# Two of eight convolution chunks leave VectorE in a decoder block: ScalarE makes the taps' products, GpSimd adds them

## What is computed

```python
y = lax.conv_general_dilated(u, conv_w[:, None, :], window_strides=(1,),
    padding=[(CONV_KERNEL - 1, 0)], dimension_numbers=('NWC', 'WIO', 'NWC'),
    feature_group_count=CONV_WIDTH)      # CONV_KERNEL = 31 taps
y = y + conv_b
y = layer_norm(y, ln_g, ln_b)            # over the 1024 channels
return jax.nn.silu(y)
```

## Time and profile before

| | |
|---|---|
| time, median of 3 runs | 1834.55 us (1831.73 to 1835.55) |
| span of the profiled execution | 1831.1 us |
| PE busy | 1786.4 us, 98% |
| VectorE busy | 1586.1 us, 87% |
| ScalarE busy | 826.3 us, 45% |
| GpSimd busy | 208.4 us, 11% |
| memory traffic | 618 MB, mean 337 GB/s |

### The profile page before, as it was taken

The page is one execution under the profiler, slowest core; times in us unless marked ns, Lnnn a source line. Parts: engine busy times, 40 slices in busy tenths (PEclk is TensorE's granted clock), DMA queues, the critical chain, the costliest instruction groups (busy, mean ns, idle before and its releaser), DMA issues.

```text
span 1831.1 us, 28933 instructions
## 1 busy us (share of the span) xinstructions
PE 1786.4 (98%) x9874; PEld 1564.5 (85%) x9874; DVE 1586.1 (87%) x2605; ACT 826.3 (45%) x1187; POOL 208.4 (11%) x193
## 2 busy tenths in 40 slices
PE   6999999998999999999999999999999999999998
PEld 6878888444999999999999999998888888888886
DVE  4668899966678999999999999998888888888887
ACT  3011222302645554333566666664555555554544
POOL 1000000110000000110122111121111111111110
PEclk9999999999999999999999999999999999999999
DMA  9998766799686677999999999999999999999994
GB/s 386 421 421 344 274 251 252 288 422 372 230 322 249 237 241 249 374 329 332 330 353 365 362 358 361 365 361 374 385 369 368 365 375 361 375 365 367 373 371 202
DMA packets 98193, 617.98 MB, mean 337 GB/s; under 512 B 13233, under 2 KB 21969, under 8 KB 26449
## 3 DMA queue, kind: packets, MB, share of 16 engines
q1 hardware_dynamic: 61456, 415.26, 59.2%
q0 software_dynamic: 25408, 184.58, 26.5%
q10 hardware_dynamic: 11266, 17.32, 2.6%
HBM read 600.26 MB, written 16.79 MB: 337 GB/s over the span
## 4 chain that ended last, share of the span: by engine, by line
PE 77%; DVE 10%; DMA 8%; issue 3%; ACT 1%; DVEq 0%; SPq 0%; ACTq 0%
PE ps L1310 31%; PE ps L960 14%; PE ps L967 9%; DMA raw<-in_w_ada 6%; PE ps L1005 6%; PE ps L1114 5%; PE ps L1168 4%; PE ps L1262 2%; PE ps L1016 2%; DVE big L1390 2%; DVE raw L1415 1%; DVE w_low L1368 1%; DMA big<-in_w_gate_f 1%; DVE big L1471 1%; DMA raw<-in_peer_v 1%
## 5 line engine op out<-in xcount | busy, mean ns | idle before, releaser
L673 ACT ACTIVATE w_hi<-raw 128x1024 fp32r<-128x1024 f32 x520 | 552.0, 1062 | 494.8 <-PE ps L1310 241.4
L1368 DVE TENSOR_TENSOR w_low<-raw,w_hi 128x1024 fp32r<-128x1024 f32 x520 | 633.4, 1223 | 92.4 <-ACT w_hi L673 85.6
L1310 PE MATMUL ps<-w_hi,a 128*128 128x512 f32 x1536 | 390.9, 390 | 2.0 <-ACT w_hi L673 2.0
L960 PE MATMUL ps<-a,w_hi 128*128 128x384 f32 x1856 | 374.1, 342 | 0.9 <-issue 0.8
L1310 PEld LDWEIGHTS ps<-w_hi,a 128*128 128x128 f32 x1536 | 288.7, 188 | 62.7 <-ACT stage L774 1.6
L960 PEld LDWEIGHTS ps<-a,w_hi 128*128 128x128 f32 x1856 | 316.0, 189 | 1.9 <-issue 1.7
L1310 PE MATMUL ps<-w_low,a 128*128 128x512 f32 x1024 | 274.8, 390 | 0.0
L967 PEld LDWEIGHTS ps<-a,w_low 128*128 128x128 f32 x1856 | 237.9, 191 | 9.2 <-DVE w_low L1368 9.0
L967 PE MATMUL ps<-a,w_low 128*128 128x192 f32 x1856 | 241.5, 272 | 3.8 <-DVE w_low L1368 3.5
L1310 PEld LDWEIGHTS ps<-w_low,a 128*128 128x128 f32 x1024 | 192.5, 188 | 40.8 <-DVE w_low L1368 0.7
L1415 DVE CUSTOM_DVE_ANT_0 raw<-raw,big 128x2048 f32<-128x2048 f32 x64 | 146.2, 2290 | 65.9 <-DMA raw<-in_w_ada 63.3
(11 more groups left out here) (225 smaller groups left out, 1670.2 us busy)
## 6 DMA issues: line engine op xcount, KB each, us to landing
raw<-in_peer_u SPq DMA_DIRECT2D x128, 1024.0 KB
raw<-in_peer_v SPq DMA_DIRECT2D x128, 1024.0 KB
early<-in_w_front SPq DMA_DIRECT2D x56, 1024.0 KB, 9.0
raw<-in_w_ada POOLq DMA_DIRECT2D x48, 1024.0 KB, 8.2
raw<-in_w_ada SPq DMA_DIRECT2D x32, 1024.0 KB, 12.6
raw<-in_peer_wq SPq DMA_DIRECT2D x16, 1024.0 KB
big<-in_w_gate_f SPq DMA_DIRECT2D x16, 1024.0 KB, 7.4
gel_saved<-stage ACTq DMA_DIRECT2D x64, 192.0 KB
```

Of the source, the lines that this page charges most:

```text
L673: act.activation(w_hi[:, h % 2, :], raw[:, s % RING, :], ACT.Copy).then_inc(hi_ready, 1)
L960: done = pe.matmul(ps[:, b % 2, 0:2 * TD].rearrange("p (m t) -> p m t", m=2), w_hi[:, ph.nth(j) % 2, k * P:(k + 1) * P], a_pair[:, kc, :, ...
L1310: done = pe.matmul(ps[:, 4 * tt + 2 * (j % 2) + n, :], a, w[:, n * 512:(n + 1) * 512], start=i is None and blk == 0 and m in (0, 2), stop= ...
L1368: dve.tensor_tensor(w_low[:, s % RING, :], raw[:, s % RING, :], w_hi[:, h % 2, :].bitcast(F32), ALU.subtract).then_inc(lo_ready, 1)
```

## The change

Chunks 6 and 7 are made by ScalarE and GpSimd. ScalarE makes for each tap two products of 128 x 256 (`upad` shifted, times the weight per channel), tap 0 straight into `convT` with the bias, the others into a ring of four `products` tiles of 128 x 512; `two_taps(m)` stands at four places of each pair. GpSimd adds a product tile to the two chunks (`add_tap`, a `tensor_tensor` of 128 x 512, 30 of them), each add behind the issue of a certain modulation block (`TAPS_BEHIND`). VectorE does the first six chunks in the pairs 0 to 2, and in the last pair ten column sums in place of 62 taps and one column sum. `MOD_ORDER` brings their blocks early. `sum_channels` waits for GpSimd's last add, too. The column sums behind the pairs are nine fewer.

```diff
-for p in range(PAIRS):
+for p in range(PAIRS - 1):
...
+SUMS_LAST_PAIR = (2, 2, 2, 2, 2)
+FFN_AT_LAST = [PAIRS - 1 + sum(SUMS_LAST_PAIR[:n]) for n in range(len(SUMS_LAST_PAIR) + 1)]
+FFN_EARLY = FFN_AT_LAST[-1]
+MOD_ORDER += [A_GATE + 12] + [A_FFN + k for k in range(FFN_AT_LAST[0], FFN_AT_LAST[2])] + [A_GATE + 13]
+MOD_ORDER += [A_FFN + k for k in range(FFN_AT_LAST[2], FFN_AT_LAST[4])] + [A_GATE + 14]
+MOD_ORDER += [A_FFN + k for k in range(FFN_AT_LAST[4], FFN_EARLY)] + [A_GATE + 15]
...
+DVE_CHUNKS = CONV_CHUNKS - 2
+TAPS_BEHIND = ((2, 4, 5, 5, 6) + (8, 9, 11, 11, 14) + (16, 17, 18, 20, 22) +
+               (24, 24, 24, 26, 26, 26, 26, 26, 28, 28, 28, 28, 28, 30))
...
+        products = region(25984, 4, 2 * T)
...
+            last_chans = convT[:, DVE_CHUNKS:CONV_CHUNKS, :].rearrange("p a b -> p (a b)")
+
+            def add_tap(j):
+
+                gp.wait_ge(tap_product, 2 * (j + 1))
+                if j > 1:
+                    gp.wait_ge(tap_added, j - 1)
+                gp.tensor_tensor(last_chans, last_chans, products[:, j % 4, :], ALU.add).then_inc(tap_added, 1)
+
             for n in range(A_GATE, N_A):
                 gp.wait_ge(mod_used, max(A_GATE, n - SLOTS + 1))
                 gp.dma_start(mod_slots[n % SLOTS], w_ada[n]).then_inc(mod_in[n % SLOTS], 16)
+                nth = n - A_GATE - SLOTS
+                if 0 <= nth < len(TAPS_BEHIND):
+                    for j in range(TAPS_BEHIND[nth - 1] if nth else 0, TAPS_BEHIND[nth]):
+                        add_tap(j + 1)
...
+            def tap_products(j):
+
+                if j == 0:
+                    act.wait_ge(glu_ready, CONV_CHUNKS)
+                    act.wait_ge(late_in, 16 * N_LATE)
+                if j >= 5:
+                    act.wait_ge(tap_added, j - 4)
+                for n in range(2):
+                    ch = DVE_CHUNKS + n
+                    if j == 0:
+                        act.activation(convT[:, ch, :], upad[:, ch, 0:T], ACT.Identity, bias=conv_v[:, 0, ch:ch + 1],
+                                       scale=conv_wt[:, ch, 0:1]).then_inc(tap_product, 1)
+                    else:
+                        act.activation(products[:, j % 4, n * T:(n + 1) * T], upad[:, ch, j:j + T], ACT.Copy,
+                                       scale=conv_wt[:, ch, j:j + 1]).then_inc(tap_product, 1)
+
+            def two_taps(m):
+
+                for j in range(2 * m, min(2 * m + 2, TAPS)):
+                    tap_products(j)
...
             for p in range(PAIRS):
                 put_qk(p, 0)
+                two_taps(4 * p)
                 if p:
                     put_aT(2 * p - 2)
                     exps(2 * p - 1)
...
+                two_taps(4 * p + 1)
                 put_qk(p, 2)
...
+                two_taps(4 * p + 2)
                 put_qk(p, 3)
...
                 exps(2 * p)
+                two_taps(4 * p + 3)
                 put_v(p)
...
-            for p in range(1, PAIRS):
+            for p in range(1, PAIRS - 1):
...
+            head_combine(HEADS - 4)
+            head_scores(HEADS - 3)
+            gate_step(12)
+            sums_last_pair(0)
+            head_combine(HEADS - 3)
+            sums_last_pair(1)
+            gate_step(13)
+            heads_variance(PAIRS - 2)
+            sums_last_pair(2)
+            heads_scale(PAIRS - 2)
+            sums_last_pair(3)
+            gate_step(14)
+            sums_last_pair(4)
+            head_scores(HEADS - 2)
+            gate_step(15)
...
-            dve.wait_ge(tap, TAPS * CONV_CHUNKS)
+            dve.wait_ge(tap, TAPS * DVE_CHUNKS)
+            dve.wait_ge(tap_added, TAPS - 1)
             sum_channels(convT)
-            column_sums(4, 5)
+            column_sums(13, 14)
```

More of the change, by code:

```diff
@@ L82 @@
 MOD_ORDER = list(range(A_GATE))
-for p in range(PAIRS):
+for p in range(PAIRS - 1):
     MOD_ORDER += [A_GATE + 4 * p, A_GATE + 4 * p + 1] + [A_FFN + p] * (p > 0)
     MOD_ORDER += [A_GATE + 4 * p + 2] + [A_FFN + p] * (p == 0) + [A_GATE + 4 * p + 3]
+SUMS_LAST_PAIR = (2, 2, 2, 2, 2)
[4 more added lines that the diff above has]
+MOD_ORDER += [A_FFN + k for k in range(FFN_AT_LAST[4], FFN_EARLY)] + [A_GATE + 15]
 MOD_GATES = len(MOD_ORDER)
-MOD_ORDER += range(A_FFN + PAIRS, N_A)
+MOD_ORDER += range(A_FFN + FFN_EARLY, N_A)
 MOD_AT = {nth: n for n, nth in enumerate(MOD_ORDER)}
+DVE_CHUNKS = CONV_CHUNKS - 2
+TAPS_BEHIND = ((2, 4, 5, 5, 6) + (8, 9, 11, 11, 14) + (16, 17, 18, 20, 22) +
+               (24, 24, 24, 26, 26, 26, 26, 26, 28, 28, 28, 28, 28, 30))
 GATE_AT = [7, 7] + [min(2 * g + 8, g + 22) for g in range(2, KC)]
@@ L280, in build_block @@
         glu_done, sig_ready, glu_ready, tap = sem("glu_done"), sem("sig_ready"), sem("glu_ready"), sem("tap")
+        tap_product, tap_added = sem("tap_product"), sem("tap_added")
         qk_evac, v_evac = sem("qk_evac"), sem("v_evac")
@@ L1552, in _, with sums_last_pair @@
                 gate_step(g0 + 3)
+            def sums_last_pair(n):
+                column_sums(FFN_AT_LAST[n], FFN_AT_LAST[n + 1])
+            head_combine(HEADS - 4)
[13 more added lines that the diff above has]
+            gate_step(15)
             head_combine(HEADS - 2)
             head_scores(HEADS - 1)
-            dve.wait_ge(tap, TAPS * CONV_CHUNKS)
+            dve.wait_ge(tap, TAPS * DVE_CHUNKS)
+            dve.wait_ge(tap_added, TAPS - 1)
             sum_channels(convT)
-            column_sums(4, 5)
+            column_sums(13, 14)
             dve.wait_ge(ln_sum, 1)
@@ L1566, in _ @@
             sum_channels(conv_sq)
-            column_sums(5, 7)
+            column_sums(14, 16)
             dve.wait_ge(ln_sum, 2)
@@ L1570, in _ @@
                 .then_inc(ln_var, 1)
-            column_sums(7, 8)
+            column_sums(16, 17)
             dve.wait_ge(ln_root, 1)
@@ L1577, in _ @@
                 dve.tensor_tensor(chans, chans, bcast_t(stat[:, 1, :], 4), ALU.mult).then_inc(ln_n, 1)
-            column_sums(8, 11)
+            column_sums(17, 20)
             heads_variance(PAIRS - 1)
-            column_sums(11, 12)
+            column_sums(20, 21)
             heads_scale(PAIRS - 1)
-            column_sums(12, 19)
+            column_sums(21, 26)
             dve.wait_ge(gate_sum_ready, 1)
@@ L1588, in _ @@
                     .then_inc(gate_made, 1)
-            column_sums(19, 22)
+            column_sums(26, 29)
             dve.wait_ge(gate_made, 4)
@@ L1602, in _ @@
                 gate_mix(0, n)
-            column_sums(22, 2 * KC - 1)
+            column_sums(29, 2 * KC - 1)
             def gate_tile(tt):
```

## The result

The changed kernel takes 1856.88 us (median; 1855.69 to 1858.76), the kernel before 1833.69 us (1831.73 to 1835.55) on the same chips: a ratio of 1.0125, 95% interval 1.0113 to 1.0137. It is 23 us slower. The profiled execution spans 1855.9 us, 24.8 more than before's.

The account below looks back on a forecast made before the run. PE was taken to pace, with the time hanging on when VectorE reaches the channel sum. 28.4 us of contention less 14.0 us free made 14.4 us: span 1845.5, median 1849.0 us, range 1833 to 1858.

Parts of the forecast that it names:

- What sets the end: When VectorE reaches the channel sum, then 327.7 us; a microsecond later there is, to first order, one at the end.
- work behind 352 us is covered: 352 to 444 us: PE runs without a stop, so nine column sums fewer on VectorE are worth nothing by themselves.
- Contention: Pairs, 28 adds ahead of VectorE's last gate step: 26.2 us of blocking plus 2.2 us of broken overlap, 28.4 us.
- DMA: Last pair, 14 w_ada blocks instead of 5: VectorE waits 0 to 3.2 us, counting only where it is not late anyway.
- turns on the read path: While a GpSimd add runs, no two-operand VectorE instruction runs; 1849.0 us, chance 0.62.
- What VectorE may lose: Ahead of the channel sum: 9.3 us of waits plus 4.7 us saved, so 14.0 us of added VectorE time are free.
- not slower if VectorE is late: VectorE's waits for PE or ScalarE, 9.3 us in all, absorb a delay since those engines are not slower.
- the 4.7 us of relief: Last pair: 24.6 us of taps leave VectorE and 19.9 us of column sums come in, saving 4.7 us.
- ScalarE and GpSimd's queue: Pairs: product groups ahead of `exps` and `put_v(3)`, and adds behind w_ada issues, are hidden and cost nothing.
- Side by side: Rival: no slowdown of VectorE or GpSimd by each other, no change, say 1834.5 us; chance 0.21.
- GpSimd is the one that waits: Rival: adds get in only in VectorE's waits and one-operand steps, delaying w_ada and add 30; 1838.5 us, chance 0.11.
- What would show it: Signs: longer taps in 150 to 320 us, PE waiting at L1031 or L1042, channel sum near 342 us, VectorE's waits gone.

Follow-up runs that it names:

- the kernel with neither: Changed kernel without GpSimd's additions and with one column sum in the last pair, ScalarE's products kept: 1833.11 us, 0.9999 against the kernel before.
- the kernel that only writes: Changed kernel with GpSimd's 30 additions replaced by fills of the same 128x512 tile, waits kept: 1842.81 us, 1.005 against the kernel before.
- the single instructions: Small kernel of its own, single VectorE instructions issued while GpSimd adds run: two SBUF operands 1.47 instead of 0.48 us.
- The kernel with late sums: Changed kernel with adds kept, one column sum in the last pair and nine back behind the pairs: 1846.51 us, 1.0069 against the kernel before.
- the kernel without adds: Changed kernel without GpSimd's 30 additions, ScalarE's products and ten early column sums kept: 1843.11 us, 1.0053 against the kernel before.
- the small kernel: Separate kernel of VectorE tap streams with GpSimd adds released into them: an add asked after the 12th of 24 taps stood 5.79 us.

## Why the prediction was right, and where it was not

**What sets the end: right.** Everything behind the channel sum moved as one. It starts 23.8 us later, PE's waits of 1.87 and 0.69 us come back at the same distance, and the span is 24.8 us longer; the last microsecond I did not look for. It holds less well for small shifts: 1.3 us earlier in the kernel with neither gave no shorter span. That work behind 352 us is covered holds as well.

**The sum was too small**: 14.4 us late at the channel sum against 23.8. Three terms are mis-sized, and two of them nearly cancel: contention 6.7 us too large, the free time 6.1 us too large. What is left is DMA.

*Contention, 28.4 us forecast, 21.7 measured.* That is each VectorE group's growth of the mean times its count in 139 to 351 us: taps 6.3, gate steps 0.8, column sums 1.1, `head_combine`'s small instructions 10.2 (L1548 from 287 to 950 ns, x7, is 4.6 of it; L1551 2.65, L1546 2.4, L1540 0.55), L1558 2.3, L1584 1.1. It makes 0.78 us an add for 28 adds, against 1.01 in the forecast. The mechanism is right: turns on the read path, shown by the kernel that only writes (484 ns a tap again) and by the single instructions. The add was taken as 1.04 us and is 1.26; the part of it that VectorE pays was taken as 0.9 and is 0.62 (0.78 of 1.26). In long runs of taps it is the add that stands, as the first one shows; that this is the whole reason is not shown. The estimate from the Trainium skill (GPSIMD Engine Reference, section 3.1: 4497 ns for 2048 columns, hence 1.12) was nearer than mine; 2048 columns took 4.49 us here. I also had the wrong instructions in mind: taps and gate steps. Over half of the loss is in small instructions, each of which can wait for a whole add.

*What VectorE may lose, 14.0 us forecast, 7.9 measured.* Its waits went from 9.3 us to 3.36 + 1.58 + 1.18 = 6.1, so they absorbed 3.2, not 9.3; with the 4.7 of the forecast that makes 7.9. The failed step is "not slower if VectorE is late": ScalarE and PE were late too. And the 4.7 us of relief lie in the last pair, while the adds of the first three pairs stop PE before that. The kernel with late sums shows it alone: 15.8 us of waits in the last pair and still 12.7 us slower. A sum of all losses against all slack is only right within the stretch between two points at which PE waits.

*DMA, 0 forecast, 8.5 us measured.* "It counts only where VectorE is not late anyway" was wrong: VectorE was late, and waited besides. I had worked out 0 to 3.2 us from slots filled in advance. As I read it, four slots are too few: loads stop when VectorE stands at another wait, and then it takes a block in 2.2 us while they arrive 3.4 to 4.4 us apart (the starts behind the five waits of the kernel without adds). The chain of waits, after, has such a block as its largest single piece in 290 to 380 us:

```profile
321.37 4.72 issue
326.10 12.29 DMA raw<-in_w_ada
```

The issue waits for a slot, and the block needs 12.29 us with the queues full. That ten early sums cost 10 us by the medians, with or without adds, and five nothing, is shown; why the slots filled in advance didn't carry VectorE is read from the traces.

The account: 21.7 + 8.5 - 7.9 = 22.3 of the 23.8 us; the rest of 1.5 us was not followed up. PE's record adds up too: 18.5 us of stops and 3.0 us at the lower clock behind the stop at 255 us make 21.5; the stretch from 294 to 348 us has a mean clock of 0.95, which is up to another 2.7. That is where PE's time went, not a second cause: ahead of the channel sum it is VectorE that is late, and PE still waits 1.87 us for it at 365.64, so the stop of 3.44 us and the low clock behind it are covered.

**ScalarE and GpSimd's queue, "nothing": wrong at the first add.** The products stand ahead of `exps` as I said, but also ahead of `put_qk`, and they wait for adds. One add that stood 22.84 us held ScalarE for 13.95 and PE for 2.57 us. For the rest of the kernel the term was right: with products and no adds the time is that of before.

**Side by side, 1834.5 us: not tested as I priced it.** It assumed no contention and the early sums. The kernel without adds is just that, and takes 1843.1: the rival's price was short by the DMA term, and even without contention the change would have been slower.

**GpSimd is the one that waits, 1838.5 us: true in part.** It happens in long runs of taps (22.84 us; 5.79 in the small kernel), but its price is not in w_ada's issue or in add 30, where I put it, but in ScalarE behind it.

**What would show it.** The taps grew, PE waits for VectorE where named (L1042 is L1093 now, and L1081 stands right ahead of L1082, which was L1031), and the channel sum came at 351 instead of 342. Waits of VectorE for w_ada were named as the sign of DMA; they are at 323 to 338 us, ahead of the last scores. An add is 1.26 us long, under the 1.5 named; its records of over 2 us are waiting. VectorE's waits before 320 us should be gone and were not (6.1 us): that sign spoke against the 14.0 us.

**The size came out inside the range (1833 to 1858), near its upper end**, since the end for a long add made room for the DMA waits that had none. That is luck. So is a part of the distance: the forecast put the median 3.45 us above the span, which compared the median with the span of another execution. A run lies 2.1 us above its own span (1857.97 and 1855.9 us), and here the median lies 1.0 us above the profiled span. The span was forecast 10.4 us too short, the median only 7.9.

## What to carry to other kernels

Moving elementwise work from VectorE to GpSimd is no gain by itself: a GpSimd instruction that reads two operands from SBUF takes turns with VectorE's two-operand work, and with its smallest scalings. Ask of each move who is full: here PE paces, so freed VectorE time was worth nothing, and every stop of PE in an early stage stays to the end however much time VectorE has later. Work that is pulled forward brings its transfers forward; count blocks per stage against what the queues bring in that stage, and expect a few slots to hide only a few blocks.

## What the runs showed of the hardware

An add of 128x512 on GpSimd is 1.26 us, of 128x2048 4.49 us, a fill of 128x512 0.52. An add against VectorE: a two-operand instruction 1.47 us instead of 0.48, a scaling of two columns 1.21 us; no wait with a PSUM operand or for a reduction; and ScalarE's copies beside one left it at 1.26. What I had given only 0.11, as a rival, is that the lock works in both directions, and over many instructions: a stream of two-operand VectorE instructions without a break keeps an add out for as long as it lasts (22.84 us in the kernel) once the add has missed its beginning; one reduction, one PSUM operand or one wait in it lets the add in, a scaling does not (each seen once). A new add gets in behind the 2nd or 4th instruction of a stream but not behind the 7th, 12th or 14th; why, is open.
